# A chunked recurrence on Trainium2: block states copied out earlier, GpSimd's gate steps held back, weight splits moved

## What is computed

```python
def step(state, inp):
    r_t, w_t, k_t, v_t, a_t, b_t = inp
    sa = jnp.einsum('bhvk,bhk->bhv', state, a_t)
    state = (state * w_t[:, :, None, :] + sa[..., None] * b_t[:, :, None, :]
             + v_t[..., None] * k_t[:, :, None, :])
    return state, jnp.einsum('bhvk,bhk->bhv', state, r_t)
...
y = ((y - mean) * lax.rsqrt(var + GN_EPS)).reshape(bsz, seq, d)
y = y * ln_w.astype(f32) + ln_b.astype(f32)
bonus = jnp.sum(rh * kh * r_k.astype(f32), axis=-1, keepdims=True) * vh
y = (y + bonus.reshape(bsz, seq, d)).astype(h.dtype)
return (y * g) @ w_o, v_first
```

## Time and profile before

| | us |
|---|---|
| median of 3 runs | 1112.14 (1108.95 to 1112.54) |
| the profiled execution's own time | 1110.59 |
| its span | 1108.4 |
| TensorE busy in the span | 1081.1 |
| VectorE busy | 812.2 |
| ScalarE busy | 553.7 |
| GpSimd busy | 47.3 |

### The profile page before, as it was taken

The page is one execution under the profiler, slowest core; times in us unless marked ns, Lnnn a source line. Parts: engine busy times, 40 slices in busy tenths (PEclk is TensorE's granted clock), DMA queues, the critical chain, the costliest instruction groups (busy, mean ns, idle before and its releaser), DMA issues.

```text
span 1108.4 us, 18637 instructions
## 1 busy us (share of the span) xinstructions
PE 1081.1 (98%) x7454; PEld 911.3 (82%) x7454; DVE 812.2 (73%) x1153; ACT 553.7 (50%) x690; POOL 47.3 (4%) x58
## 2 busy tenths in 40 slices
PE   8999999999999998999999999999999999999998
PEld 7887888888877778787788888798967888999996
DVE  4665445538579788888999988999997967555554
ACT  5645633436365534553444456366545656444443
POOL 0000000000000440101111000000000000000000
PEclk9999999999999998999999999999999999999999
DMA  9695456453334321859999964374621553464633
GB/s 331 206 261 183 168 189 215 150 204 114 114 123 145 95 48 41 302 170 364 338 334 357 323 218 120 116 239 130 208 101 34 195 179 124 163 218 153 220 120 113
DMA packets 138093, 205.86 MB, mean 186 GB/s; under 512 B 19544, under 2 KB 95597, under 8 KB 138030
## 3 DMA queue, kind: packets, MB, share of 16 engines
q1 hardware_dynamic: 130596, 177.63, 49.4%
q0 software_dynamic: 6560, 25.19, 6.6%
q10 hardware_dynamic: 874, 2.15, 0.5%
HBM read 202.33 MB, written 1.57 MB: 184 GB/s over the span
## 4 chain that ended last, share of the span: by engine, by line
PE 82%; DVE 12%; ACT 2%; DMA 2%; issue 1%; SPq 0%; ACTq 0%; DVEq 0%
PE ps L756 23%; PE ps L758 23%; PE ps L757 23%; DVE wl L2538 2%; PE ps L982 2%; DMA raw<-in_ab_w_in 1%; PE ps L1639 1%; PE ps L1200 1%; PE ps L833 1%; PE ps L1115 1%; PE ps L1467 1%; PE ps L1114 1%; PE ps L1139 1%; PE ps L1621 1%; DVE wide L2652 1%
## 5 line engine op out<-in xcount | busy, mean ns | idle before, releaser
L2538 DVE TENSOR_TENSOR wl<-raw,wh 128x2048 fp32r<-128x2048 f32 (+2 forms) x154 | 345.4, 2248 | 98.8 <-ACT wh L1762 98.3
L756 PE MATMUL ps<-wh,xh 128*128 128x512 f32 (+3 forms) x856 | 335.6, 392 | 3.7 <-DVE wl L2538 2.3
L758 PE MATMUL ps<-wl,xh 128*128 128x512 f32 (+3 forms) x856 | 328.3, 384 | 0.0
L757 PE MATMUL ps<-wh,xl 128*128 128x512 f32 (+3 forms) x856 | 327.9, 383 | 0.0
L1762 ACT ACTIVATE wh<-raw 128x2048 fp32r<-128x2048 f32 (+2 forms) x154 | 286.9, 1878 | 54.4 <-PE ps L758 28.4
L756 PEld LDWEIGHTS ps<-wh,xh 128*128 128x128 f32 x856 | 160.9, 188 | 38.3 <-issue 3.4
L758 PEld LDWEIGHTS ps<-wl,xh 128*128 128x128 f32 x856 | 160.8, 188 | 31.7
L757 PEld LDWEIGHTS ps<-wh,xl 128*128 128x128 f32 x856 | 161.0, 188 | 30.2 <-issue 1.0
L756 PE MATMUL ps<-wh,gh 128*128 128x512 f32 x288 | 112.9, 392 | 1.7 <-issue 0.9
L757 PE MATMUL ps<-wh,gl 128*128 128x512 f32 x288 | 112.2, 390 | 0.0
L758 PE MATMUL ps<-wl,gh 128*128 128x512 f32 x288 | 112.1, 389 | 0.0
(11 more groups left out here) (450 smaller groups left out, 1309.1 us busy)
## 6 DMA issues: line engine op xcount, KB each, us to landing
wide<-in_w_ada POOLq DMA_DIRECT2D x24, 1024.0 KB, 10.4
raw<-in_ffn_w_gate SPq DMA_DIRECT2D x44, 512.0 KB, 4.7
raw<-in_ffn_w_up SPq DMA_DIRECT2D x44, 512.0 KB, 5.8
raw<-in_ffn_w_down SPq DMA_DIRECT2D x22, 1024.0 KB, 5.1
raw<-in_w_mlp_in SPq DMA_DIRECT2D x16, 1024.0 KB, 7.1
raw<-in_w_mlp_out SPq DMA_DIRECT2D x16, 1024.0 KB, 5.0
raw<-in_w_in SPq DMA_DIRECT2D x16, 512.0 KB, 4.9
raw<-in_w_in SPq DMA_DIRECT2D x8, 1024.0 KB, 5.0
```

The source lines that it names most:

```text
L756: pe.matmul(o, lh, rh, start=start, stop=False)
L757: pe.matmul(o, ll, rh, start=False, stop=False)
L758: return pe.matmul(o, lh, rl, start=False, stop=stop)
L2538: v.tensor_tensor(wl[:, s, 0:width], raw[:, s, 0:width], f32(wh[:, s, 0:width]), ALU.subtract).then_inc(lo_ready[s], 1)
```

## The change

- `wkv.T` is counted twice in each `flip`, after the first eight and after all sixteen transposes. `ar_out` waits for the first count, `bk_out` for the second.
- GpSimd's gate steps of the first half of the heads wait for the first pair's sums (`wkv.y1` at 2), those of the second half for the end of the second inversion (`wkv.near` at 2).
- VectorE, at the end of the first pair: both split halves of `first` leave their places around `q_out`. `state_out` of both groups goes ahead of `inverse_out(2)` and `inverse_out(3)`, after a wait for the inversion's last step, whose working space it overwrites. The four split halves of `first` and `second` follow.

```diff
@@ -136,7 +136,7 @@
     "pe_12": (("cum", 1), ("conv_mm", 8)),
     "pe_18": (("ffn0.out", 3), ("ffn1.out", 3), ("ukv.k", 1), ("out.t", 4), ("mlp.out", 3)),
     "pe_13": (("rk_T", 1), ("pc_T", 1), ("at.o", 8)),
-    "pe_14": (("wkv.T", 4), ("cmean", 1)),
+    "pe_14": (("wkv.T", 8), ("cmean", 1)),
     "pe_15": (("wkv.gram_b", 4), ("cvar", 1)),
     "pe_16": (("wkv.gram_ts", 4), ("ym.T", 4)),
     "pe_17": (("wkv.gram_k", 4), ("pre2.T", 4)),
@@ -728,6 +728,8 @@
                 o, n0 = slice(512 * hh, 512 * hh + 512), B("fold") + 8 + 4 * hh
                 pool.wait_ge(S("gate_out"), B("gate_out") + 2 * (hh + 1))
                 if hh:
+                    pool.wait_ge(S("wkv.near"), B("wkv.near") + 2)
+                else:
                     pool.wait_ge(S("wkv.y1"), B("wkv.y1") + 2)
                 for t in range(NT):
                     bt = BTERM(W, side, gh_plain, gl_plain, hh, t)
@@ -1210,7 +1212,8 @@
                     c = HEAD(g, HEADS(g, q))[0]
                     o = (q % 2) * SEQ
                     turn(bank(g, q // 2)[:, o:o + P], aa[:, c:c + P])
-                    turn(bank(g, q // 2)[:, o + P:o + SEQ], rr[:, c:c + P])
+                    m = turn(bank(g, q // 2)[:, o + P:o + SEQ], rr[:, c:c + P])
+                m.then_inc(S("wkv.T"), 1)
                 if g == 0:
                     pe.wait_ge(S("rkv"), B("rkv") + 12)
                 for q in range(4):
@@ -2121,11 +2124,16 @@
                 b = 4 * (g % 2) + i
                 return ps[:, b:b + 2, 0:n]
 
-            def out_of_two(sem, b, dst, done, n=512, at=0, before=None):
+            def turned_out(b, dst, done):
 
                 def step(g):
-                    if before:
-                        act.wait_ge(S("wkv." + before), B("wkv." + before) + g + 1)
+                    act.wait_ge(S("wkv.T"), B("wkv.T") + 2 * g + (1 if dst == "ar" else 2))
+                    act.activation(tmps[g][dst].rearrange("p (b n) -> p b n", b=2), banks(g, b), ACT.Copy).then_inc(S("wkv." + done), 1)
+                return step
+
+            def out_of_two(sem, b, dst, done, n=512, at=0):
+
+                def step(g):
                     act.wait_ge(S("wkv." + sem), B("wkv." + sem) + g + 1)
                     act.activation(tmps[g][dst].rearrange("p (b n) -> p b n", b=2), ps[:, 4 * (g % 2) + b:4 * (g % 2) + b + 2, at:at + n],
                                    ACT.Copy).then_inc(S("wkv." + done), 1)
@@ -2180,7 +2188,7 @@
                 act.wait_ge(S("gn_var"), B("gn_var") + 2 * hh + t + 1)
                 act.activation(gvar[:, o], gvar[:, o], ACT.Sqrt).then_inc(S("gn_std"), 1)
 
-            ar_out, bk_out = out_of_two("T", 0, "ar", "ar"), out_of_two("T", 2, "bk", "bka")
+            ar_out, bk_out = turned_out(0, "ar", "ar"), turned_out(2, "bk", "bka")
             mt_out, r1_out = out_of_pair("mt", "mt_m", "mtc"), out_of_two("r1", 2, "r1", "r1c")
             r2_out, r4_out = out_of_one("r2", 2, "r2", "r2a", 512), out_of_one("r4", 0, "r4", "r4a", 512)
             ar_out(0)
@@ -2956,7 +2964,7 @@
                 return ap.rearrange("p (b n) -> p b n", b=2)
 
             def bk_out(g):
-                v.wait_ge(S("wkv.T"), B("wkv.T") + g + 1)
+                v.wait_ge(S("wkv.T"), B("wkv.T") + 2 * g + 2)
                 v.tensor_copy(two(tmps[g]["bk"]), banks(g, 2)).then_inc(S("wkv.bk"), 1)
 
             def pair_of(name, g):
@@ -3208,21 +3216,20 @@
                 r4_out(g + 1)
                 if g == 0:
                     near_last()
-                    split_in_place(first, 0)
                 else:
                     gated(0, 0)
                 q_out(g)
-                if g == 0:
-                    split_in_place(first, 1)
-                else:
+                if g == 2:
                     gated(0, 1)
                 q_out(g + 1)
+                v.wait_ge(S("wkv.near"), B("wkv.near") + 2)
+                state_out(g)
+                state_out(g + 1)
                 if g == 0:
                     inverse_out(2)
                     inverse_out(3)
-                state_out(g)
-                state_out(g + 1)
-                if g == 0:
+                    split_in_place(first, 0)
+                    split_in_place(first, 1)
                     split_in_place(second, 0)
                     split_in_place(second, 1)
 
```

## The result

| | before | changed |
|---|---|---|
| median, us | 1111.18 | 1113.74 |
| range of 22 runs each, us | 1108.95 to 1113.55 | 1109.42 to 1117.86 |
| profiled execution, us (span) | 1110.59 (1108.4) | 1115.88 (1114.0) |

The ratio is 1.0021, with a 95% interval of 1.0011 to 1.0031: a little slower. (Ratios here are estimated from the single runs; they aren't the quotients of the two medians.) The forecast was 0.3 us of gain. The spread says more than the median: the runs of before form one group, those of the changed kernel seem to form two, 10 runs from 1109.4 to 1112.0 and 12 from 1113.7 to 1117.9. The profiled execution is from the upper group.

The account below looks back on a forecast made before the run. TensorE was taken to bound four fifths of the span, its longest recurrence wait 2.40 us before the second `gram_v`. Terms 0 + 0 + 0 - 0.3 us, put on the median 1112.14, gave 1111.8 us; range 1108.6 to 1114.6.

Parts of the forecast that it names:

- Halves: Transposes signalled in halves: round-two copies end up to 0.9 us sooner, counted at nothing because the second inversion's load covers it.
- First gate steps: GpSimd's steps held until `y1`: `inverse_out(0)` 2.0 us shorter, counted at nothing because the second inversion's load covers it.
- Second gate steps: GpSimd's steps held until the second inversion ends: done by 414.3, some 2.5 us to spare before ScalarE's third-block split; nothing.
- States and splits: Second round: `gram_v` 2.4 us sooner, but `carry(0, 1)` behind four split halves takes back 2.1; -0.3 us.
- The second: Rival: clock falls at the wait for `carry(0, 1)` and costs more, up to +2.9 us, 1115.0; chance 0.22.
- the new wait: TensorE's forecast wait for `carry(0, 1)` before the second `next_state`, from 418.4 to 422.4, 4.0 us long.
- The third: Rival: the clock doesn't fall at all in the recurrence, -0.9 us, 1111.2; chance 0.18.
- The fourth rival: The second inversion starts as soon as VectorE is free, -3.3 us, 1108.8; chance 0.10.
- the range given: Forecast range for the whole kernel's time, 1108.6 to 1114.6 us.
- the slower side: Whole kernel measurably slower, by more than about 0.3%: upper end of the clock-falls-later case with scatter; chance 0.09.

Follow-up runs that it names:

- experiment 1: The kernel before with the transposes signalled in halves and nothing else of the change; 1115.33 us, ratio 1.003.
- experiment 2: The changed kernel without the halves, its other parts kept; 1111.38 us, ratio 0.9999.
- experiment 3: The kernel before with 16 more warm-up products at its start, the recurrence untouched; 1111.99 us, ratio 1.0004.
- experiment 8: The changed kernel without the halves, with `carry` ahead of later split halves and `gkv_out(3)` ahead of ScalarE's third-block split; 1110.34 us, ratio 0.999.
- experiment 7: The kernel before with states ahead of the second inverses and split halves behind, no halves, no held gate steps; 1111.37 us, ratio 1.0004.
- experiment 10: The changed kernel without the halves, with the third block's weight load issued ahead of the second inverses' store; 1112.08 us, ratio 1.0008.

## Why the prediction was wrong

**Halves: the step that failed.** The prediction counted them at nothing because the second inversion's load hides what they bring, and of that load and its store it said "nothing in the change moves these". The first half held: TensorE's wait of 0.73 us became 0.30, and nobody gained by it. The second failed, though no issue of the SP queue was moved. The step looked at what stands before the transfers in their queue, not at what else the DMA engines carry in those microseconds. TensorE reaches its 2150th matmul record, about where the load of the next instructions begins in all these profiles, 0.9 us sooner in relation to the store, and the load's place goes from 1.94 us behind the store's issue to 1.16. That cost 2.85 us in the second inversion's input (landed 12.6 us behind the store's issue instead of 9.8), 1.07 of it up to the second store's issue and 1.78 in that store, and 1.8 us of half rate behind the longer wait. These make 4.65; where the 0.35 down to the measured 4.3 came back was not traced. With 12 of 22 runs in the upper group, the medians are 2.6 us apart. Experiments 1, 2 and 3 show it: the halves alone bring it, the change without them doesn't have it, and shifted code brings it without the change.

**First gate steps: right.** `inverse_out(0)` went from 2.75 to 0.76 us, and in the kernel without halves the second inversion still begins on its load, at 396.04. That the steps would still stretch the inversion's last product is right for that kernel too, 1.47 us as before (first line below). In the changed kernel's profile the late product comes after the steps and takes 1.08 us (second line):

```profile
406.69 1.47 DVE L3015 TENSOR_TENSOR wide<-near_u,near_p 128x512 f32<-128x512 f32 x1
```

```profile
412.35 1.08 DVE L3016 TENSOR_TENSOR wide<-near_u,near_p 128x512 f32<-128x512 f32 x1
```

**Second gate steps: right.** ScalarE waited for the third block's load and not for GpSimd:

```profile
424.48 1.91 ACT L1832 ACTIVATE wh<-wl_plain 128x2048 fp32r<-128x2048 f32 x1 [2.17 <-DMA wl_plain<-in_rwkv_w_o]
```

**States and splits: right in size, not in all of its reasons.** In the kernels without halves `gram_v` starts at 415.30 and 415.34 with no wait (forecast 415.7), `carry` at 420.93 and 420.99 (421.5), the second `next_state` at 421.96 and 422.01 (422.4); these runs stand about 0.3 us earlier than the one the forecast was made on. The forecast of -0.3 us lies inside both intervals (0.9999 and 1.0004). What it did not see is that a second cause stands in the same place: of the idle time before `next_state`, 1.98 us in the kernel without halves is TensorE waiting for its own instructions, so moving `carry` alone could gain almost nothing (experiment 8).

**The rivals.** The second, a fall of the clock at the new wait, happened in experiment 2's kernel (0.50 from 419.7 to 426.5), after 1.98 us idle, and in the changed kernel (0.50 from 427.7 to 431.1), after 2.81. The third, no fall, happened in experiment 7, after 3.64 us. Experiments 2 and 7 have the same median (1111.38 and 1111.37). By the rule that the prediction took from the Trainium skill ("TensorE: Matmul & The Clock Gate", "HAM oscillation"), the work behind a gap starts cold; behind two of these gaps it did, and behind a longer one it did not, so from this trace nobody could have told which. The fall that cost time was at a third place, in the wait ahead of the products of `y1` (0.50 from 403.8 to 410.7), which is 0.35 us long in the kernel before. The fourth rival didn't happen: nothing let the inversion start sooner.

**The numbers.** 1113.74 lies in the range given, and 0.2% is less than the 0.3% that the prediction called measurable; with 22 runs of each, the interval excludes no change. The chance of 0.09 for the slower side rested on the clock alone. A rival "a transfer on the path gets company" had no place in it.

## What to carry to other kernels

Where a chain goes out to memory and back by small transfers, ask what else the DMA engines do in those microseconds; TensorE's instruction loads are among it, and their place follows from how many products stand before. A kernel whose runs fall into two groups some 4 us apart may have such a near miss; compare the issue-to-landing times of the same transfer in several runs before suspecting the code that was changed, and don't take a run's total for a sign of it. An edit that wins idle time on an engine that nobody waits for can still move its instruction loads; test each such part alone before it goes in with others.

## What the runs showed of the hardware

In the recurrence an instruction load of 16 KB takes 0.9 to 1.6 us. A store of 128 packets of 1 KB, done in 1.7 us when no such load begins in its first 1.3 us, took 2.8 to 3.7 us when one began 0.5 to 1.2 us behind its issue; eight of its packets come late. The other way about, an instruction load among 1 MB of weights began at 417.40 (experiment 2) where one just ahead of them began at 414.33 (experiment 7), some 3 us apart, and TensorE stood still for 1.98 us, 2.81 in the changed kernel, with nothing in the profile to release it ("issue"). Both were unexpected, and the cause of both shows only in the DMA part of the trace.

The Trainium skill, "Advanced Engine Details and Errata", section "ISA Cache", states lines of 16 KB for 256 instructions, and only two of them. The trace agrees: a matmul record comes with a weight load, so it is two instructions, and the thirteen loads in the recurrence of the kernel before come 125 records apart in the mean (92 to 162, and 187 at its load of 1 MB); in the changed kernel and in experiment 8 TensorE stopped 252 and 246 records, some 500 instructions, after the beginning of the last load that came in time. The same section gives 128 KB for TensorE; by its own line size that would be, as an estimate, some 1000 records, and these two stops don't agree with it. That these loads and the kernel's own transfers hold each other up is what the rows above show.

Last, the granted clock: 3.64 us idle left it at 1.00 in experiment 7, and 3.57 us idle in the same place in experiment 10 was followed by 0.50. What decides between the two is open.
